# Router on transposes of the raw residual, and routing of the first tiles inside the output projection

## What is computed

```python
mix = concat([attn, pooled]) @ w_out
h = layer_norm(ALPHA * x + mix, ln1_g, ln1_b)
pg = softmax(h @ w_r1 + b_r1); g = argmax(pg)           # 4 groups
lf = (h @ w_r2 + b_r2).reshape(T, 4, 8)[g]              # 8 experts in the group
pe, e = top_k(softmax(lf), 2)
weights = pg_top * pe / sum(pe)
y = sum over the two experts: weight * (silu(h @ w_gate) * (h @ w_up)) @ w_down
out = layer_norm(ALPHA * h + y, ln2_g, ln2_b)
```

## Time and profile before

| | us |
|---|---|
| median of 3 runs | 585.3 (584.33 to 605.53) |
| profiled execution | 584.9 |
| its span, first to last instruction | 583.1 |
| busy in the span: TensorE | 505.0 (87%) |
| VectorE | 229.5 (39%) |
| ScalarE | 150.5 (26%) |
| GpSimd | 161.2 (28%) |
| mean granted TensorE clock | 0.933 of full |

### The profile page before, as it was taken

One profiled execution on the slowest core, in us unless ns is written; L12 is line 12 of the kernel. 1 busy time (PEld: TensorE's weight loads), 2 busy tenths in 40 slices (PEclk: granted clock), 3 DMA queues, 4 the chain that ended last, 5 costly groups with the idle time before them and its releaser, 6 DMA issues.

```text
span 583.1 us, 6186 instructions
## 1 busy us (share of the span) xinstructions
PE 505.0 (87%) x2202; PEld 286.7 (49%) x2202; DVE 229.5 (39%) x562; ACT 150.5 (26%) x313; POOL 161.2 (28%) x158
## 2 busy tenths in 40 slices
PE   5999999999799998999748798999877897779591
PEld 4586675756464456888643333443333333333230
DVE  2101482898789753245560211221111101011387
ACT  3333323532236765032230110211111110111032
POOL 2243342387624773033350011121111101100000
PEclk9999999999899999999857898999989988889876
DMA  9944468004019200892487799999999999999803
GB/s 320 307 51 51 52 167 272 30 1 144 1 42 360 106 0 1 338 419 108 188 321 276 306 397 422 420 421 420 420 419 420 419 422 419 421 420 378 325 8 144
DMA packets 42440, 148.04 MB, mean 254 GB/s; under 512 B 11284, under 2 KB 15892, under 8 KB 30120
## 3 DMA queue, kind: packets, MB, share of 16 engines
q1 hardware_dynamic: 37992, 139.71, 63.6%
q0 software_dynamic: 4320, 7.82, 3.6%
q10 hardware_dynamic: 96, 0.08, 0.0%
HBM read 137.16 MB, written 18.35 MB: 267 GB/s over the span
## 4 chain that ended last, share of the span: by engine, by line
PE 54%; SPq 15%; DMA 13%; DVE 9%; issue 4%; POOL 2%; ACT 2%; POOLq 0%; DVEq 0%; ACTq 0%
PE bank L1304 17%; SPq L489 10%; PE bank L1469 8%; PE bank L1409 8%; DMA wgu<-in_w_up_dram 5%; SPq L492 5%; DMA xe<-h_rows,row_from 4%; PE bank L1493 3%; PE bank L1277 3%; PE bank L1371 3%; PE bank L1349 3%; PE bank L1324 2%; PE bank L1455 2%; PE bank L1362 2%; DMA yg<-y_rows 2%
## 5 line engine op out<-in xcount | busy, mean ns | idle before, releaser
L1469 PE MATMUL bank<-wgu,xeT 128*64 128x512 f32 x512 | 126.4, 650 | 23.3 <-DMA wgu<-in_w_up_dram 22.5
L1469 PEld LDWEIGHTS bank<-wgu,xeT 128*64 128x64 f32 x512 | 42.2, 149 | 97.3 <-issue 93.5
L709 POOL DMA_INDIRECT y_rows<-ye,row_to x14 | 14.2, 1011 | 180.5 <-PE bank L1455 120.6
L1493 PE MATMUL bank<-wd,actT 128*64 128x512 f32 x256 | 60.9, 618 | 1.4 <-ACT actT L863 1.4
L1135 DVE TENSOR_TENSOR act_row<-bank,sil 128x256 f32<-128x256 f32 x16 | 6.8, 425 | 127.9 <-ACT sil L856 127.8
L611 POOL TENSOR_TENSOR ring_low<-ring,wt_high 128x1024 fp32r<-128x1024 f32 x12 | 28.6, 2386 | 54.6 <-ACT wt_high L736 54.6
L856 ACT ACTIVATE sil<-bank 128x256 f32<-128x256 f32 x16 | 6.1, 384 | 141.3 <-PE bank L1469 141.3
L1493 PEld LDWEIGHTS bank<-wd,actT 128*64 128x64 f32 x256 | 20.5, 142 | 37.7 <-issue 37.7
L1304 PE MATMUL bank<-xT_high,ring_low 128*128 128x512 f32 x128 | 32.7, 397 | 0.0
L1149 DVE COPY xeT<-bank 128x512 f32<-128x512 f32 x16 | 11.1, 691 | 52.1 <-PE bank L1455 52.1
L1349 PE MATMUL bank<-kT,qT 64*128 64x128 f32 (+3 forms) x64 | 25.9, 485 | 5.1 <-DVE nmx L1001 4.3
(11 more groups left out here) (203 smaller groups left out, 775.5 us busy)
## 6 DMA issues: line engine op xcount, KB each, us to landing
wgu<-in_w_gate_dram SPq DMA_DIRECT2D x32, 1024.0 KB, 22.0
wgu<-in_w_up_dram SPq DMA_DIRECT2D x32, 1024.0 KB, 26.3
wd<-in_w_down_dram SPq DMA_DIRECT2D x32, 1024.0 KB, 28.6
ring<-in_w_in_dram SPq DMA_DIRECT2D x5, 2048.0 KB, 14.0
wo<-in_w_out_dram SPq DMA_DIRECT2D x2, 2048.0 KB, 8.0
y_rows<-zero SPq DMA_DIRECT2D x1, 4096.0 KB, 21.7
yg<-y_rows SPq DMA_DIRECT2D x8, 512.0 KB, 9.1
bias_rows<-brow SPq DMA_DIRECT2D x1, 2560.0 KB
```

What stands on the lines that cost most here:

```text
L1469: ins = pe.matmul(bank[2 + i][half_rows(n), :], xeT[i][:, k, half_rows(n)], wgu[slots[n]][:, :, k, :], start=k == 0, stop=k == KD - 1)
L1493: ins = pe.matmul(bank[4 + c][half_rows(n), :], actT[i][:, m, half_rows(n)], wd[PAIR_SLOTS[p % 3][n]][:, m, 512 * c:512 * c + 512], start= ...
```

## The change

- The residual stays in the `x_again` buffers; `x_again` of tile t+2 is loaded when tile t is normalised, not when its residual is made. `out_ps`, `hT_ps`, `hT_ready` and `res_ready` count halves, and VectorE takes residual and statistics of a half as soon as its 24 matmuls are done.
- TensorE transposes the raw residual. ScalarE alone copies the transposes, as two instructions of 512 columns. The router's weights are multiplied by `ln1_g` once (VectorE); the sums over all rows of these and of weights times `ln1_b` come from two reductions and one matmul with ones. `route` makes the logits as product times 1/std, plus mean term (`wr_mean`).
- ScalarE normalises after the copies, from `x_again` to h, in two halves. GpSimd scales and shifts when `norm_ready` comes, and doesn't wait for the transposes.
- TensorE's order: transposes of tile t-1 at (0, 4) of tile t, router at (1, 0), `ranks` of tiles 0 to 2 at (1, 6) of tile 3. VectorE's order: `route(t-1)`, for t = 3 also `place(0..2)`, then `residual(t)`, `factors(t)`.
- Tile 3 of h is stored by ScalarE's queue; SyncE waits for `h_ready` of all tiles ahead of expert 4's down part.

```diff
@@ SyncE
             for t in range(2):
-                sp.wait_ge(res_ready, t + 1)
+                sp.wait_ge(norm_ready, t + 1)
                 load_x_again(t + 2)
                 store_h(t)
-            sp.wait_ge(out_ps, NT)
+            sp.wait_ge(out_ps, 2 * NT)
             load_expert(3)
             store_h(2)
             load_gate_up(4, PAIR_SLOTS[2][0], gu_in_slot[PAIR_SLOTS[2][0]])
-            store_h(3)
+            sp.wait_ge(h_ready, NT)
             load_down(4, PAIR_SLOTS[2][0], down_in_slot[PAIR_SLOTS[2][0]])
@@ GpSimd
                 pool.wait_ge(norm_ready, t + 1)
-                pool.wait_ge(hT_ps, t + 1)
                 link(pool.tensor_tensor(h[:, t, :], h[:, t, :], g1[:, :], ALU.mult))
@@ ScalarE
             def transposed_h(t):
-                act.wait_ge(hT_ps, t + 1)
                 if t >= 2:
                     act.wait_ge(router_ps, t - 1)
-                for k in range(KD // 2):
...
+                for i in range(2):
+                    act.wait_ge(hT_ps, 2 * t + i + 1)
+                    act.activation(hT[t % 2][:, 4 * i:4 * i + 4, :], bank[4 + i][:, :].rearrange("p (k t) -> p k t", k=4), ACT.Copy).then_inc(hT_ready, 1)
...
+                for i in range(2):
+                    ins = act.activation(h[:, t, 512 * i:512 * i + 512], x_again[t % 2][i][:, :], ACT.Identity, bias=nmr[:, t:t + 1], scale=rstd[:, t:t + 1])
+                ins.then_inc(norm_ready, 1)
             for t in range(NT):
-                if t >= 1:
-                    transposed_h(t - 1)
-                normalise(t, t, h[:, t, :])
-            transposed_h(NT - 1)
+                transposed_h(t)
+                normalise(t)
+            act.wait_ge(h_ready, NT)
+            act.dma_start(h_dram[P * (NT - 1):P * NT, :], h[:, NT - 1, :]).then_inc(h_stored, 16)
@@ VectorE
+            def residual(t):
+
+                dve.wait_ge(x_again_in[t % 2], 32 * (t // 2 + 1))
                 for i in range(2):
+                    dve.wait_ge(out_ps, 2 * t + i + 1)
+                    hv = x_again[t % 2][i][:, :]
+                    dve.scalar_tensor_tensor(out=hv, in0=hv, scalar=ALPHA, in1=bank[(2 if t % 2 == 0 else 0) + i][:, :],
+                                             op0=ALU.mult, op1=ALU.add).then_inc(res_ready, 1)
+                    dve.wait_ge(res_ready, 2 * t + i + 1)
+                    link(dve.bn_stats(stats[:, i, :], hv))
...
+                dve.scalar_tensor_tensor(out=wr_mean[:, :], in0=wr_sum[:, :], scalar=nmr[:, t:t + 1], in1=wr_const[:, :], op0=ALU.mult,
+                                         op1=ALU.add).then_inc(dve_chain, 1)
...
-                link(dve.tensor_tensor(gl[:, t, 0:GROUPS], ps[:, 0:GROUPS], br[:, 0:GROUPS], ALU.add))
-                dve.tensor_tensor(lf[:, :], ps[:, GROUPS:], br[:, GROUPS:], ALU.add).then_inc(router_sb, 1)
+                link(dve.scalar_tensor_tensor(out=gl[:, t, 0:GROUPS], in0=ps[:, 0:GROUPS], scalar=rstd[:, t:t + 1], in1=wr_mean[:, 0:GROUPS],
+                                              op0=ALU.mult, op1=ALU.add))
+                dve.scalar_tensor_tensor(out=lf[:, :], in0=ps[:, GROUPS:], scalar=rstd[:, t:t + 1], in1=wr_mean[:, GROUPS:],
+                                         op0=ALU.mult, op1=ALU.add).then_inc(router_sb, 1)
...
+            link(dve.tensor_tensor(wr_bias[:, :, :], wr[:, :, :], bT[:, :].unsqueeze(2).to_broadcast([P, KD, GROUPS + NE]), ALU.mult))
+            link(dve.tensor_tensor(wr[:, :, :], wr[:, :, :], gT[:, :].unsqueeze(2).to_broadcast([P, KD, GROUPS + NE]), ALU.mult))
+            for i, part in enumerate((wr, wr_bias)):
+                ins = dve.tensor_reduce(out=wr_part[:, i, :], in_=part[:, :, :].rearrange("p k n -> p n k"), axis=AX.X, op=ALU.add)
+            ins.then_inc(wr_ready, 1)
...
+            for t in range(NT):
+                if t >= 1:
+                    route(t - 1)
+                if t == NT - 1:
+                    dve.wait_ge(rank_ps, 1)
+                    place(0, NT - 1, bank[3][:, 0:NE * (NT - 1)])
+                residual(t)
+                factors(t)
@@ TensorE
             def transpose_h(t):
...
+                for i in range(2):
+                    pe.wait_ge(res_ready, 2 * t + i + 1)
+                    for k in range(4):
+                        ins = pe.transpose(bank[4 + i][:, P * k:P * k + P], x_again[t % 2][i][:, P * k:P * k + P], ident[:, :])
+                    ins.then_inc(hT_ps, 1)
...
+                        if (t, i, k) == (0, 1, 0):
+                            pe.wait_ge(wr_ready, 1)
+                            pe.matmul(bank[7][:, 0:2 * (GROUPS + NE)], ones[:, :], wr_part[:, :, :], start=True, stop=True).then_inc(wr_sum_ps, 1)
+                        if t >= 1 and (i, k) == (0, 4):
+                            transpose_h(t - 1)
+                        if t >= 1 and (i, k) == (1, 0):
+                            router(t - 1)
+                        if t == NT - 1 and (i, k) == (1, 6):
+                            pe.wait_ge(earlier_ready, NT - 1)
+                            ranks(0, NT - 1, bank[3][:, 0:NE * (NT - 1)]).then_inc(rank_ps, 1)
```

More of the change, by code:

```diff
@@ L216, in layer_kernel @@
         std = small("std", [1])
-        rstd = small("rstd", [1])
-        nmr = small("nmr", [1])
+        rstd = small("rstd", [NT])
+        nmr = small("nmr", [NT])
         iota_e = small("iota_e", [NE])
@@ L250, in layer_kernel @@
         square_sum, std2, rstd2 = [at(name, wpool_at + 320 + 32 * i, [NT]) for i, name in enumerate(("square_sum", "std2", "rstd2"))]
+        wr_sum, wr_const, wr_mean = [at(name, wpool_at + 512 + 160 * i, [GROUPS + NE]) for i, name in enumerate(("wr_sum", "wr_const", "wr_mean"))]
+        wr_part = at("wr_part", wpool_at + 1024, [2, GROUPS + NE])
         rank1 = small("rank1", [NT, NE])
@@ L338, in layer_kernel @@
         hT_ready = sem("hT_ready")
-        hT_ready_dve = sem("hT_ready_dve")
+        wr_ready = sem("wr_ready")
+        wr_sum_ps = sem("wr_sum_ps")
+        wr_sum_sb = sem("wr_sum_sb")
         router_ps = sem("router_ps")
@@ L1048, in transposed_h, with factors @@
[L1048 to L1056, removed]
+            def factors(t):
+                dve.wait_ge(std_ready, t + 1)
+                link(dve.reciprocal(rstd[:, t:t + 1], std[:, :]))
+                link(dve.tensor_scalar(nmr[:, t:t + 1], mv[:, 0:1], rstd[:, t:t + 1], -1.0, ALU.mult, ALU.mult))
+                dve.sem_inc(scale_ready, 1)
+                dve.scalar_tensor_tensor(out=wr_mean[:, :], in0=wr_sum[:, :], scalar=nmr[:, t:t + 1], in1=wr_const[:, :], op0=ALU.mult,
+                                         op1=ALU.add).then_inc(dve_chain, 1)
+                n[0] += 1
+                dve.wait_ge(dve_chain, n[0])
@@ L1117, in place @@
                 dve.tensor_tensor(rank1[:, t0:t1, :], hot_rank[:, t0:t1, 0, :], hot_rank[:, t0:t1, 1, :], ALU.add).then_inc(rank1_ready, 1)
-            transposed_h(NT - 1)
-            dve.wait_ge(rank_ps, 1)
-            place(0, NT - 1, bank[3][:, 0:NE * (NT - 1)])
+            dve.wait_ge(wr_sum_ps, 1)
+            dve.tensor_copy(wr_sum[:, :], bank[7][:, 0:GROUPS + NE]).then_inc(wr_sum_sb, 1)
+            dve.tensor_tensor(wr_const[:, :], bank[7][:, GROUPS + NE:2 * (GROUPS + NE)], br[:, :], ALU.add).then_inc(wr_sum_sb, 1)
+            dve.wait_ge(wr_sum_sb, 2)
+            for t in range(NT):
[6 more added lines that the diff above has]
+                factors(t)
             route(NT - 1)
@@ L1380, in transpose_h @@
             def transpose_h(t):
-                pe.wait_ge(norm_ready, t + 1)
                 if t >= 1:
[L1383 to L1387, removed]
+                    pe.wait_ge(hT_ready, 2 * t)
+                for i in range(2):
[3 more added lines that the diff above has]
+                    ins.then_inc(hT_ps, 1)
             def router(t):
-                pe.wait_ge(hT_ready, t + 1)
-                pe.wait_ge(hT_ready_dve, t + 1)
+                pe.wait_ge(hT_ready, 2 * t + 2)
+                if t == 1:
+                    pe.wait_ge(wr_sum_sb, 2)
                 if t >= 2:
@@ L1396, in router @@
                 ins.then_inc(router_ps, 1)
[L1398 to L1412, removed]
             def ranks(t0, t1, out):
@@ L1427, in lists @@
                 return ins
+            for t in range(NT):
+                if t >= 2:
+                    pe.wait_ge(res_ready, 2 * t - 2)
+                for i in range(2):
+                    for k in range(KD):
+                        cols, cols_out = slice(P * t, P * t + P), slice(512 * i, 512 * i + 512)
+                        w_low_k = wo_low[k // 4][:, k % 4, cols_out]
+                        parts = ((mix_high[:, k, cols], wo_high[k][:, cols_out]), (mix_low[:, t, k, :], wo_high[k][:, cols_out]), (mix_high[:, k, cols], w_low_k))
+                        if (t, i, k) == (0, 1, 0):
[8 more added lines that the diff above has]
+                            ranks(0, NT - 1, bank[3][:, 0:NE * (NT - 1)]).then_inc(rank_ps, 1)
```

(6 more changed lines are left out.)

24 lines of the change are left out of this document (6 added, 18 removed).

## The result

The changed kernel took **610.15 us** in the median of four runs (608.27 to 612.32) against 584.91 of the kernel before: ratio 1.0436, 95% interval 1.0379 to 1.0493 (the ratio sets the four against the three runs of the kernel before at 584.3 to 585.3; its fourth took 605.5). The forecast was 586.5 with a range to 591. The profiled execution took 612.3, its span is 610.6.

What follows compares the result with a forecast made beforehand. The expert stage's start, then its bytes, were taken to bound the kernel. The first gather landing 1.2 us later, carried as 1.5, made 584.9 + 1.5 = 586.4, forecast as 586.5 us, range 582 to 591.

Steps and rivals of the forecast that it cites:

- 584.9 + 1.5: Whole kernel: profiled time before plus the later landing of the first gather, carried as 1.5 us, giving 586.4.
- part 4: Last store of h and DMA queue: store lands at 303.5, just behind the row list, a new wait for the gather.
- Rival (b): Start of expert stage: last store and first gather queue behind the expert weights, +3.7, 588.6 us; chance 0.17.
- part 3: Tile 3 on VectorE, from residual through routing: row list ready at 303.1, before 302.75.
- The block: Routing beside GpSimd's work on h: L1070, first step with two SBUF inputs, waits until the running GpSimd instruction ends.
- The longer projection: TensorE in the projection: added router, weight sums, ranks and a stall move its end from 283.2 to 287.0.
- the new stall of TensorE: Ahead of the ranks inside tile 3's projection: TensorE waits 0.85 us for tile 2's delayed routing.
- the chain of 5.5 us: Tile 3, residual's start to transposes: 5.5 us of statistics, factors and normalising gone, 4.25 us given back elsewhere.
- The preparations of the weights: VectorE at the projection's start: four preparations, 1.2 to 2.8 us together, hidden before the matmul that waits for them.
- The idea that computation gains nothing: Last tile's computation up to the row list: list at 303.1 against 302.75 before, so no gain.
- the first paragraph's shift "one to one": Expert stage: bytes behind 308 us are unchanged, so a shift of the first gather's landing reaches the end in full.
- rival (c): Expert stage: the bytes hide the shift if requests of pairs 0 to 2 run full either way, 585.0 us; chance 0.13.

Runs made afterwards that it cites:

- the changed kernel with the filled stretch: Changed kernel plus one unused 128x384 matmul at TensorE's 0.87 us idle stretch in attention unit 19: 588.3 to 589.6 us in six runs, ratio 1.0066.

## Why the prediction was wrong

**The step that failed first is the unspoken one.** The sum was "584.9 + 1.5" and took everything ahead of the projection as given; a fall of the clock in the attention stands in it at nothing, without a reason. Measured, the stretch ahead of the projection took 255.6 us and not 233.0: 22.6 of the 27.4 us. The earlier trace rows begin at 233 us; a stage that the change leaves alone was read for no risk of its own. The three runs shown had one of 605.5 us, and the forecast called 2% what a measurement can tell without asking what that run was. A term "clock falls in the attention, +20 us, in some executions" could have been had from it. No case of the forecast reached 591. That all four of the first runs fell on the long side was chance as far as the runs tell: 2 of the next 8 did.

**The store and the DMA queue (part 4)** was mis-sized: "I take 303.5" is 70.5 from the projection's start, measured 74.4. The store took 8.8 us and not 5.2. The stretch from 310 to 330 us holds 20 us at 367 GB/s, so 7.3 MB, which is all that was requested from the projection's end up to the store: the store landed when nearly all of it had moved. In the kernel before the same store took 5.5 us, with expert 4's down part requested behind it in the same queue; here that 1 MB was requested 0.01 us ahead of it (321.25, 321.26) in the other queue. With all of expert 4 held back the store took 3.9 us. No run separates the change of queue from the order of the two requests. In place of the "+1.5" the change costs 3.5. Rival (b), store and gather behind the weights at 588.6, is what happened; measured 588.9. Its chance was 0.17.

**The list (part 3)** was put at 303.1, so 70.1; it came at 72.4. The block was taken for instructions with two SBUF inputs, L1070 of the kernel before (L1072 after). It strikes the step ahead, which makes `pen` and has one SBUF tensor input, and a cast of two elements (1.73 us), while a cast of one element beside L691 keeps its 0.15. And not only GpSimd's `h` instructions block, its memsets do too: 319.24 to 323.04 covers the rest of the add and both memsets, 3.8 us for a step of 0.24. The run with the memsets early takes just 1.8 us of it away (list 70.6), which is near the forecast's 70.1. The Trainium skill, "SBUF — State Buffer", section "Who interferes with whom", says that tensor_scalar and cast can enter a two-port mode, if their operands meet its conditions, and in it contend with GpSimd. The trace agrees with that: `pen` (a tensor_scalar) takes 1.08 to 3.80 against 0.24, the cast 1.73 against 0.17.

**What held.** The longer projection (54.0 forecast, 54.3 measured), the new stall of TensorE (0.85, 1.04), place without its block (1.95, 308.44 to 310.30 is 1.86), the chain of 5.5 us from residual to transposes gone, router 3 at half clock (3.60, 3.63), the request of the last store (65.3, 65.7). The preparations of the weights were hidden, and their matmul took 0.17 on TensorE's chain, not 0.4. From the request of expert 5 to the end it is 275.2 us in the changed kernel with the filled stretch, 274.9 in the kernel before, within the 1 us that the forecast allowed. The idea that computation gains nothing was right: what the change takes from the chain of the last tile it puts into the projection and in front of the last residual.

**Carried to the end:** the 3.6 us at the first gather in the changed kernel with the filled stretch (78.8 against 75.2 in the kernel before with it) arrive as 3.5. Where the gather came early but bytes were held back (expert 4), they did not arrive whole. So the first paragraph's shift "one to one" held for this change, and rival (c), in which the bytes hide it, did not decide it.

**What stays open.** Why the clock falls in one execution and not in the next at the same idle stretch was not settled; the clock stayed up in all 38 executions with an extra matmul there, by the idle time that it fills or by the work that it adds. The pair behind the stretch starts at 195.24 to 195.65 us in the four traces with the fall, and at 194.40, 194.56, 194.60, 195.87 and 196.87 in the five without it and without a matmul there: that its place in time decides is possible and not shown.

## What to carry to other kernels

Read the clock column over the whole span and the spread of the run times before judging a change by its median: a stage that the change doesn't touch can be worth more than the change, and four runs may all fall on one side. If a short idle stretch of TensorE stands where the clock falls, one unused matmul that fits into it is a cheap test, and here the cure. When work of VectorE moves beside GpSimd's, price what that does to its shortest instructions (0.24 us became up to 3.80 here); and when several transfers wait behind one event, count the bytes that it sets free before counting instructions.

## What the runs showed that was not expected

- TensorE's granted clock fell to 1.2 GHz right behind 0.87 us of idle time, after 45 us in which TensorE had been 39.5 us busy, and it stayed there from 196 to about 244 us, 47 us, though TensorE was called fully busy.
- A VectorE instruction on 32 elements waited 3.6 us for three GpSimd instructions, the last two of them memsets that stand without a gap behind the first: it did not get its turn between them. Between the two `h` instructions of tile 0, which leave 0.07 us, the same step did (276.39 + 1.08 is 277.47, the second starts at 277.51).
- A store of 0.5 MB from ScalarE's queue, requested 9 us behind the last of 5.8 MB on SyncE's, took 8.8 us (7.8 in another execution): it landed 1.0 us behind the last of those weights and 1.4 us ahead of the 1 MB requested in the same instant. The Trainium skill, "DMA: Bandwidth & Descriptors", section "Issuing engines are not separate DMA queues", says that they run on the same engines and interleave; the trace agrees with that, and the other queue did not bring the store past the weights requested before it.
